# Two start addresses in the partition are rounded up to a multiple of 128 bytes

## The reference, cut to what matters

```python
gt, up = split_cols(h @ w_gate_up[i], (D_FF, D_FF))        # D_FF = 2816
x = x + (jax.nn.silu(gt) * up) @ w_down[i]                 # "0"
h = swiglu(rms_norm_2(x, ffn1_pre[l]), ffn1_w_gu[l], ffn1_w_down[l])   # "1", and "2" at the end
```

## Time and profile before

| | |
|---|---|
| median of three runs | 2215.86 us |
| span of the profiled execution, first to last instruction | 2212.5 us |
| TensorE matmul busy | 2159.1 us, 98% of the span |
| TensorE weight loads busy | 1800.3 us, 81% |
| VectorE busy | 1257.0 us, 57% |
| ScalarE busy | 823.4 us, 37% |
| GpSimd busy | 190.0 us, 9% |
| granted TensorE clock, mean | 0.998 of full speed |

### The profile page before, as it was taken

The page is one execution under the profiler, slowest core; times in us unless marked ns, Lnnn a source line. Parts: engine busy times, 40 slices in busy tenths (PEclk is TensorE's granted clock), DMA queues, the critical chain, the costliest instruction groups (busy, mean ns, idle before and its releaser), DMA issues.

```text
span 2212.5 us, 34964 instructions
## 1 busy us (share of the span) xinstructions
PE 2159.1 (98%) x14262; PEld 1800.3 (81%) x14262; DVE 1257.0 (57%) x1891; ACT 823.4 (37%) x1313; POOL 190.0 (9%) x138
## 2 busy tenths in 40 slices
PE   7999999999999999999999999999999999999998
PEld 5877788787888888888888888888897688888887
DVE  4789889898755554444532554443237835444323
ACT  5345434355454333332222542332233544223222
POOL 0100222203323001000000100000000110000000
PEclk9999999999999999999999999999999999999999
DMA  4242111122112243333322323323222122333321
GB/s 162 79 133 77 59 45 44 54 77 63 32 47 72 92 143 128 95 95 95 117 92 78 124 69 100 97 95 114 92 70 67 39 61 74 96 102 96 114 92 52
DMA packets 56171, 189.89 MB, mean 86 GB/s; under 512 B 6256, under 2 KB 8688, under 8 KB 56048
## 3 DMA queue, kind: packets, MB, share of 16 engines
q1 hardware_dynamic: 53168, 182.88, 25.9%
q10 hardware_dynamic: 2880, 5.24, 0.6%
HBM read 178.66 MB, written 9.44 MB: 85 GB/s over the span
## 4 chain that ended last, share of the span: by engine, by line
PE 80%; issue 9%; DVE 8%; ACT 2%; POOL 0%; DMA 0%; ACTq 0%; DVEq 0%; POOLq 0%
PE pg L657 68%; PE pC L919 4%; PE pB L919 1%; DVE w_lo L1869 1%; DVE cpad L1949 1%; DVE sacc L2091 1%; PE pC L761 1%; ACT w_hi L1273 1%; PE pA L979 1%; PE pB L688 1%; DVE a_lo L1928 0%; PE pA L735 0%; PE pC L735 0%; PE pB L719 0%; DVE tb L2215 0%
## 5 line engine op out<-in xcount | busy, mean ns | idle before, releaser
L657 PE MATMUL pg<-a_hi,w_hi 128*128 128x512 f32 (+1 forms) x1920 | 745.9, 388 | 14.3 <-ACT ptile L1363 4.4
L657 PE MATMUL pg<-a_lo,w_hi 128*128 128x512 f32 (+1 forms) x1920 | 738.5, 385 | 0.0
L657 PE MATMUL pg<-a_hi,w_lo 128*128 128x512 f32 (+1 forms) x1920 | 736.2, 383 | 0.0
L1869 DVE TENSOR_TENSOR w_lo<-w_raw,w_hi 128x1024 fp32r<-128x1024 f32 (+3 forms) x299 | 382.7, 1280 | 385.8 <-ACT w_hi L1273 385.1
L1273 ACT ACTIVATE w_hi<-w_raw 128x1024 fp32r<-128x1024 f32 (+3 forms) x299 | 329.7, 1103 | 649.4 <-PE pg L657 638.6
L657 PEld LDWEIGHTS pg<-a_hi,w_hi 128*128 128x128 f32 x1920 | 361.4, 188 | 90.2 <-DVE a_lo L1928 8.7
L657 PEld LDWEIGHTS pg<-a_hi,w_lo 128*128 128x128 f32 x1920 | 361.3, 188 | 68.3 <-issue 1.4
L657 PEld LDWEIGHTS pg<-a_lo,w_hi 128*128 128x128 f32 x1920 | 361.5, 188 | 67.4 <-issue 0.9
L657 PE MATMUL pg<-h_hi,w_hi 128*128 128x512 f32 (+1 forms) x572 | 215.7, 377 | 0.6 <-DVE w_lo L1869 0.6
L657 PE MATMUL pg<-h_hi,w_lo 128*128 128x512 f32 (+1 forms) x572 | 214.5, 375 | 0.0
L657 PE MATMUL pg<-h_lo,w_hi 128*128 128x512 f32 (+1 forms) x572 | 212.4, 371 | 0.0
(11 more groups left out here) (374 smaller groups left out, 2295.2 us busy)
## 6 DMA issues: line engine op xcount, KB each, us to landing
w_raw<-in_w_gu SPq DMA_DIRECT2D x132, 512.0 KB, 3.5
w_raw<-in_w_in SPq DMA_DIRECT2D x74, 512.0 KB, 3.5
w_raw<-in_w_dn SPq DMA_DIRECT2D x48, 704.0 KB, 4.1
spill_g<-tmp ACTq DMA_DIRECT2D x16, 256.0 KB, 2.0
w_raw<-in_w_co SPq DMA_DIRECT2D x8, 512.0 KB, 3.8
w_raw<-in_w_do SPq DMA_DIRECT2D x8, 512.0 KB, 3.6
w_raw<-in_w_wo SPq DMA_DIRECT2D x8, 512.0 KB, 4.0
w_raw<-in_w_pg SPq DMA_DIRECT2D x8, 512.0 KB, 3.5
```

Of the source, the lines that this page charges most:

```text
L657: ins = pe.matmul(dst[:, cols], w_of(w, n % 2, k), b(k)[:, cols], start=first and q == 0, stop=last and q == len(todo) - 1)
L1869: dve.tensor_tensor(w_lo[:, n % 2, 0:c], w_raw[:, n % 4, 0:c], w_hi[:, n % 2, 0:c].bitcast(F32), ALU.subtract).then_inc(S("w_lo"), 1)
```

## The change

Before R_OFF is taken, and again before O_OFF is taken, the running address is rounded up to a multiple of 128 bytes. No instruction is added, removed or moved in any queue.

```diff
@@ in build, after ost
         ost = at("ost", 8 * NC, shape=[P, 8 * NC])
+        base[0] += -base[0] % 128
         R_OFF = base[0]
```

## The result

The changed kernel takes 2224.7 us (median of four runs, 2224.18 to 2227.03) against 2215.89 us for the one before, whose median has a fourth run in it by now: a ratio of 1.0044, with a 95% interval of 1.0032 to 1.0056. (The ratio is estimated from the single runs; the quotient of the medians is 1.0040.) It is slower by 8.8 us. The forecast was 2212.9 us, and the range ended at 2217.0.

The account below looks back on a forecast made before the run. TensorE's distance between matmul starts was taken to bound the kernel. Full-width matmuls on h gave -3.4 us, half-width +0.4 us, all else 0: 2215.86 - 3.0 = 2212.9 us, range 2211.0 to 2217.0 us.

Parts of the forecast that it names:

- What bounds the kernel: Three feed-forwards, unbroken matmul pieces of 357, 334 and 334 us: only the distance between TensorE's matmul starts counts.
- Full-width matmuls on h: Feed-forwards' 1452 matmuls on h: each gives back 2.35 ns if h takes a's distance, -3.4 us.
- rival three: Moving-to-stationary address distance counts, 128 bytes is bad; h, o and yb slow down: +5.0 us, 2220.8 us; chance 0.08.
- Half-width matmuls: 264 matmuls of 256 columns on h: each costs 2.2 ns more, 198 on the path, +0.4 us.
- Writers, DMA, small matmuls: ACT and DVE writes, ptile and pl transfers, mixer's small matmuls: 0 us each, the small matmuls within 0.3 us either side.
- if o or yb leaves 389 ns: Trace test on o and yb durations: then a coarser grain or the distance to the weights counts, not the multiple of 128.
- Rival one: Matmuls on h: the address is not the cause of their slower rate, time stays at 2215.9 us; chance 0.26.

Follow-up runs that it names:

- third experiment: R_OFF and O_OFF both rounded up to a multiple of 256 bytes from the first tile, against the kernel before: ratio 0.9987, 2212.13 us against 2214.99.

## Why the prediction was wrong

*What bounds the kernel*: right. The loss came in the stretches named, as a larger distance between starts, with TensorE never idle.

*Full-width matmuls on h, "if h takes the distance of a"*: this is the step that failed. The difference of 229.0 to 226.6 ns was real, and it does come from the address: at distance 0 it goes (third experiment, 226.7 ns). But I let a multiple of 128 count as a's address. It was not: h went to 128 modulo 256 from the weights, and the runs show 233.3 ns there. The term of -3.4 us became +6.4 us. For the address that a really has, the forecast's whole sum holds: -3.0 us was forecast, and the third experiment, with h at distance 0, measured -2.9 us.

*The second rounded address*: I had O_OFF's move by 128 bytes in the front of this document and in rival three, but the forecast's own sum has no term for it. It cost 2.5 us, shown by moving it alone.

*Half-width matmuls*: the sign was right for distance 0 (120.0 ns). At 128 h's halves measured 118.8 ns, 5.94 us for 50 distances, which adds 0.2 us or less.

*Writers, DMA, small matmuls*: nothing to be seen. ACT's h_hi takes 633 ns where it took 632, the two transfers 9.0 and 9.5 us where they took 8.9 and 9.6, and the score matmuls have a mean of 592 ns before and after.

*Rival three* was the right mechanism, with its place (h, o and yb, and nothing on a) and its cause (distance to the weights), and its test, "if o or yb leaves 389 ns", is what the trace showed. It got 0.08. Its price was too small: 231.0 ns from unit "ab" in place of 233.3, so +5.0 us in place of the 8.8 us measured. What was held against it, that "ab" has weight loads of another width, made a row from the one stretch with other distances count for nothing. The better argument was in the layout: a, o and yb shared a multiple of 256 and not only one of 128, so that the rows of before never showed a fast operand at 128. The forecast rested on a distance that no row of a full-sized product had.

*Rival one*, the address not being the cause, is refuted by the third experiment. The Trainium skill's grain of 16 bytes in "SBUF — State Buffer", section "SBUF: two separate sides", gives no difference between any two distances of the table, since all are whole lines; the measurement of 226.7 against 233.3 ns decides. The Trainium skill's two independent read ports in "TensorE: Matmul & The Clock Gate", section "Step-by-step: what each phase is for", would leave no room for what moving the weights alone did; the measurement, +32.5 us, decides here too.

## What to carry to other kernels

Where matmuls with a weight load each follow one another without a gap, compare the distances between starts by operand, and then the addresses of moving operand and weights against each other, not each one against a round number. In this kernel a difference that was a multiple of 256 bytes was the fast one, and a pad in front of one region moved every region behind it. Before rounding one address up, list which others move with it, and ask for each whether any row shows an operand at the new place.

## What the runs showed of the hardware that I had not expected

- A matmul of 512 columns with its own weight load starts every 226.7 ns at distance 0 and every 233.3 ns at most others, at the same granted clock of 1.00. With 256 columns the order is turned round: 120.0 ns at distance 0, 118.8 at 128, 117.8 at 64.
- The effect isn't monotonic: 32 bytes cost 6.6 ns and 64 bytes 2.3.
- It depends on moving operand and weights together: moving w_lo alone took two gaps of three from about 227 ns to 232.7 and 234.0, moving h_lo or h_hi alone cost 7 ns a triple, both together 20.
- Why the distance matters isn't shown by any run here, and neither is whether a distance of 0 stays the best in a kernel with other shapes.
